# A head's attention values on TensorE: one group of eight matmuls over up to 512 queries in place of two groups, four and eight, over 256

## The reference, cut to what matters

```python
def one_block(args):                     # causal_attention, mixer B; mixer A is alike
    qb, i = args                         # 128 queries of block i
    s = jnp.einsum('bqhd,bkhd->bhqk', qb, k) * scale
    s = jnp.where((kpos[None, :] <= qpos[:, None])[None, None], s, -jnp.inf)
    pr = jax.nn.softmax(s, axis=-1)
    return jnp.einsum('bhqk,bkhd->bqhd', pr.astype(v.dtype), v)
```

## Time and profile before

| | us |
|---|---|
| median of 3 runs (1789.79 to 1790.21) | 1790.18 |
| profiled execution | 1791.9 |
| its span, first to last instruction | 1790.1 |
| PE busy in the span | 1769.0 (99%) |
| DVE busy | 1259.2 (70%) |
| ACT busy | 951.9 (53%) |
| POOL busy | 848.6 (47%) |

### The profile page before, as it was taken

How to read it: one execution, slowest core, us unless ns; L and a number is a source line. 1 busy time by engine, 2 the same in 40 slices (tenths; PEclk the granted TensorE clock), 3 DMA queues, 4 the chain that set the end, 5 groups by cost and what they waited for, 6 DMA issues and landing times.

```text
span 1790.1 us, 28924 instructions
## 1 busy us (share of the span) xinstructions
PE 1769.0 (99%) x10094; PEld 1545.7 (86%) x10094; DVE 1259.2 (70%) x2445; ACT 951.9 (53%) x1873; POOL 848.6 (47%) x458
## 2 busy tenths in 40 slices
PE   9999999999999999999999999999999999999997
PEld 9888888878879999988898888888787799999886
DVE  6279989867788888513363899897778788884133
ACT  4544877844465555422244557787444555654222
POOL 5446942354443434354434578334443434444542
PEclk9999999999999999999999999999999999999998
DMA  5332111123333333233333321111233333332431
GB/s 191 98 95 90 60 59 60 60 72 101 99 118 95 108 106 102 89 118 106 96 100 101 96 81 60 60 60 61 81 106 94 106 107 100 114 95 83 130 106 59
DMA packets 47078, 166.64 MB, mean 93 GB/s; under 512 B 5472, under 2 KB 5728, under 8 KB 46944
## 3 DMA queue, kind: packets, MB, share of 16 engines
q1 hardware_dynamic: 46080, 163.60, 29.5%
q10 hardware_dynamic: 864, 1.28, 0.2%
HBM read 162.76 MB, written 2.10 MB: 92 GB/s over the span
## 4 chain that ended last, share of the span: by engine, by line
PE 72%; issue 12%; DVE 8%; POOL 5%; ACT 2%; DMA 0%; DVEq 0%; POOLq 0%; SPq 0%; ACTq 0%
PE banks L1124 19%; PE banks L1126 18%; PE banks L1125 18%; POOL sb_wl L595 5%; PE banks L1175 3%; PE banks L1177 3%; PE banks L1176 3%; PE banks L1231 2%; PE banks L1281 2%; DVE sb_work L1613 1%; DVE sb_top L1611 1%; DVE banks L1676 1%; PE banks L1262 1%; DVE sb_pbuf L1635 1%; PE banks L1261 1%
## 5 line engine op out<-in xcount | busy, mean ns | idle before, releaser
L595 POOL TENSOR_TENSOR sb_wl<-sb_wraw,sb_wh 128x1024 fp32r<-128x1024 f32 x223 | 546.0, 2452 | 660.7 <-ACT sb_wh L723 640.9
L1124 PE MATMUL banks<-sb_xh,sb_wh 128*128 128x512 f32 (+1 forms) x1184 | 428.9, 362 | 4.0 <-POOL sb_wl L595 3.0
L1126 PE MATMUL banks<-sb_xh,sb_wl 128*128 128x512 f32 (+1 forms) x1184 | 412.0, 348 | 0.0
L1125 PE MATMUL banks<-sb_xl,sb_wh 128*128 128x512 f32 (+1 forms) x1184 | 411.5, 348 | 0.0
L723 ACT ACTIVATE sb_wh<-sb_wraw 128x1024 fp32r<-128x1024 f32 x215 | 227.2, 1058 | 298.9 <-PE banks L1126 184.5
L1124 PEld LDWEIGHTS banks<-sb_xh,sb_wh 128*128 128x128 f32 x1184 | 224.9, 190 | 30.1 <-issue 5.1
L1126 PEld LDWEIGHTS banks<-sb_xh,sb_wl 128*128 128x128 f32 x1184 | 224.4, 190 | 29.3
L1125 PEld LDWEIGHTS banks<-sb_xl,sb_wh 128*128 128x128 f32 x1184 | 225.3, 190 | 16.1
L1124 PE MATMUL banks<-sb_t_hi,sb_wh 128*128 128x256 f32 x640 | 181.2, 283 | 0.0
L1125 PE MATMUL banks<-sb_t_lo,sb_wh 128*128 128x256 f32 x640 | 181.2, 283 | 0.0
L1126 PE MATMUL banks<-sb_t_hi,sb_wl 128*128 128x256 f32 x640 | 181.2, 283 | 0.0
(11 more groups left out here) (350 smaller groups left out, 3987.0 us busy)
## 6 DMA issues: line engine op xcount, KB each, us to landing
sb_wraw<-in_weights SPq DMA_DIRECT2D x264, 512.0 KB, 3.5
sb_wraw2a<-in_weights SPq DMA_DIRECT2D x20, 512.0 KB, 3.5
sb_wraw2b<-in_weights SPq DMA_DIRECT2D x20, 512.0 KB, 4.5
sb_u<-in_x SPq DMA_DIRECT2D x8, 256.0 KB, 6.3
out<-sb_u SPq DMA_DIRECT2D x8, 256.0 KB, 2.1
sb_praw<-in_ple ACTq DMA_DIRECT2D x2, 512.0 KB, 4.3
sb_par<-in_params ACTq DMA_DIRECT2D x2, 98.5 KB, 3.1
sb_rope_tmp<-in_freq ACTq DMA_DIRECT2D x1, 24.0 KB, 4.3
```

The costliest lines, as they stand in the source:

```text
L595: nc.gpsimd.tensor_tensor(wl[:, slot(t), :], wraw[:, t % 2, :], wh[:, slot(t), :].bitcast(F32), ALU.subtract).then_inc(lo_ready, 1)
L1124: nc.tensor.matmul(out, wh_, xh_, start=start, stop=False, skip_group_check=onto)
L1125: nc.tensor.matmul(out, wh_, xl_, start=False, stop=False, skip_group_check=onto)
L1126: return nc.tensor.matmul(out, wl_, xh_, start=False, stop=stop, skip_group_check=onto)
```

## The change

A head's value work becomes one group, numbered by the head (`hd`), over all four query blocks. There is one pair of turned buffers, each of 1664 used columns, in which key block `b` holds the queries from block `b` on, next to each other: block `b` starts at column 512 x `b` and has 512 - 128 x `b` columns. So one matmul takes key block `b` with all its queries.

The group stands in slot 4 x head + 6, after the first third of the gate work and ahead of the turn of the next head's unit 0, which writes into the same buffers. ACT's copy of the group's half (step `value part`) stands where the value step was, behind the second third. The copy L781 and the low parts L1649 of a head wait until the previous head's group has been run. The copy and the addition behind the group become one each over 64 x 512 in place of two over 64 x 256. The addition's wait for `tapped` moves from head 4 to head 8.

```diff
+        head, whole = (slot - VALUE_LAG) // NT, slot >= VALUE_LAG and (slot - VALUE_LAG) % NT == NT - 1
+        if whole:
+            steps.append(("value", head))
         if TURN_LAG <= slot < UNITS + TURN_LAG:
             steps.append(("turn", slot - TURN_LAG))
         steps += [("part", p) for p in left[given + shares[0]:given + shares[0] + shares[1]]]
         if slot in PREP and PREP[slot][0] == "B":
             steps.append(("prep keys", PREP[slot]))
-        if slot >= VALUE_LAG and (slot - VALUE_LAG) % 2:
-            steps.append(("value", (slot - VALUE_LAG) // 2))
+        if whole:
+            steps.append(("value part", head))
...
-        pt_h = [sb("pt_h0", A0 + 119808, [P, 2, 256], F32R), sb("pt_h1", A0 + 99328, [P, 4, 256], F32R)]
-        pt_l = [sb("pt_l0", A0 + 121856, [P, 2, 256], F32R), idx_r[:, :, 0:256]]
-        low_part = sb("low_part", A0 + 123904, [P, 2, 256])
+        pt_h = sb("pt_h", A0 + 128000, [P, 5 * PT], F32R)
+        pt_l = sb("pt_l", A0 + 134656, [P, 5 * PT], F32R)
+        low_part = sb("low_part", A0 + 123904, [P, S])
...
+        def turned_blocks(buffer, n):
+
+            qt = n % NT
+            return buffer[:, P * qt:P * qt + PT * (qt + 1)].rearrange("p (b q) -> p b q", q=PT)[:, :, 0:P]
...
                 def turned_probabilities(n):
-                    qt, half = n % NT, n // 2 % 2
+                    qt, head = n % NT, n // NT
                     arrived("turn", n)
-                    if n >= 4:
-                        act.wait_ge(value_ready, layer * PAIRS + (n // 2 - 1))
-                    dst = pt_h[half][:, 0:qt + 1, P * (qt % 2):P * (qt % 2) + P]
+                    if head >= 1:
+                        act.wait_ge(value_ready, layer * HEADS + head)
+                    dst = turned_blocks(pt_h, n)
...
-                def value(m):
-                    hd, half = m // 2, m % 2
-                    diagonal = 2 * half + 1
-                    pe.wait_ge(prob_low, units + (2 * m + 2))
+                def value(hd):
+                    pe.wait_ge(prob_low, units + (NT * hd + NT))
...
-                    passes = [(0, pt_h), (diagonal, pt_h), (diagonal, pt_l)]
-                    passes += [(b, pt) for b in range(1, diagonal) for pt in (pt_h, pt_l)] + [(0, pt_l)]
+                    high, low = pt_h, pt_l
+                    passes = [(0, high)] + [(b, pt) for b in (3, 1, 2) for pt in (high, low)] + [(0, low)]
                     for i, (b, pt) in enumerate(passes):
-                        q0 = P if b == diagonal else 0
                         v = ukv_r[:, b, hd * P:hd * P + P] if hd < BH else idx_r[:, b, G_VA - AD:G_VA + AD]
-                        last = nc.tensor.matmul(psum[:, bank, q0:256], v, pt[half][:, b, q0:256], start=(i == 0),
-                                                stop=(i == len(passes) - 1))
+                        last = nc.tensor.matmul(psum[:, bank, P * b:S], v, pt[:, (PT + P) * b:PT * b + S],
+                                                start=(i == 0), stop=(i == len(passes) - 1))
...
                 def turned_lows(n):
-                    qt, half = n % NT, n // 2 % 2
+                    qt = n % NT
                     dve.wait_ge(turn_out, turns + (TURN_AT[("turn", n, "")] + 1))
-                    at = slice(P * (qt % 2), P * (qt % 2) + P)
+                    if n >= NT:
+                        dve.wait_ge(value_ready, layer * HEADS + n // NT)
...
-                    if slot >= NORM_LAG and (slot - NORM_LAG) % 2:
-                        combine((slot - NORM_LAG) // 2)
+                    if slot >= NORM_LAG and (slot - NORM_LAG) % NT == NT - 1:
+                        combine((slot - NORM_LAG) // NT)
```

More of the change, by code:

```diff
@@ L119 @@
 PREP |= {UNITS // 2 + 8 * p - 3: ("A", p) for p in range(AH // 2)}
-PAIRS = UNITS // 2
+HEADS = UNITS // NT
+PT = 3 * P
 Y_SPLIT = {57 + c: c for c in range(4)}
@@ L774, in turned_probabilities, with value_part @@
                 def turned_probabilities(n):
-                    qt, half = n % NT, n // 2 % 2
+                    qt, head = n % NT, n // NT
                     arrived("turn", n)
-                    if n >= 4:
-                        act.wait_ge(value_ready, layer * PAIRS + (n // 2 - 1))
-                    dst = pt_h[half][:, 0:qt + 1, P * (qt % 2):P * (qt % 2) + P]
+                    if head >= 1:
+                        act.wait_ge(value_ready, layer * HEADS + head)
+                    dst = turned_blocks(pt_h, n)
                     src = psum[:, BANK_AT[("turn", n, "")], 0:width(qt)].rearrange("p (b q) -> p b q", q=P)
                     nc.scalar.activation(dst, src, ACT.Copy).then_inc(turn_out, 1)
[L783 to L788, removed]
+                def value_part(hd):
+                    act.wait_ge(value_ready, layer * HEADS + (hd + 1))
+                    if hd >= 1:
+                        act.wait_ge(value_out, layer * HEADS + hd)
+                    own, other = (slice(0, AD), slice(AD, P))[::1 if hd % 2 == 0 else -1]
+                    nc.scalar.activation(low_part[own, :], psum[other, BANK_AT[("value", hd, "")], :],
                                          ACT.Copy).then_inc(part_out, 1)
@@ L808, in attention @@
                         exponentials(n)
-                    elif kind == "value":
+                    elif kind == "value part":
                         value_part(n)
@@ L820, in attention @@
                             act.wait_ge(turn_out, turns + (TURN_AT[("prep", ("A", 3), "")] + 1))
-                            act.wait_ge(value_out, layer * PAIRS + PAIRS // 2)
+                            act.wait_ge(value_out, layer * HEADS + BH)
                         nc.scalar.activation(yh[1][:, c], yb[:, c], ACT.Copy).then_inc(y_high, 1)
@@ L934, in _ @@
                 attention(layer, first)
-                act.wait_ge(value_out, layer * PAIRS + PAIRS)
+                act.wait_ge(value_out, layer * HEADS + HEADS)
                 for c in range(4):
@@ L1223, in bank_for @@
                         else:
-                            pe.wait_ge(value_out, layer * PAIRS + (before[1] + 1))
+                            pe.wait_ge(value_out, layer * HEADS + (before[1] + 1))
                     return BANK_AT[(kind, n, part)]
@@ L1274, in value @@
                         pe.wait_ge(va_low, layer + 1)
-                    bank = bank_for("value", m)
-                    passes = [(0, pt_h), (diagonal, pt_h), (diagonal, pt_l)]
-                    passes += [(b, pt) for b in range(1, diagonal) for pt in (pt_h, pt_l)] + [(0, pt_l)]
+                    bank = bank_for("value", hd)
+                    high, low = pt_h, pt_l
+                    passes = [(0, high)] + [(b, pt) for b in (3, 1, 2) for pt in (high, low)] + [(0, low)]
                     for i, (b, pt) in enumerate(passes):
-                        q0 = P if b == diagonal else 0
                         v = ukv_r[:, b, hd * P:hd * P + P] if hd < BH else idx_r[:, b, G_VA - AD:G_VA + AD]
-                        last = nc.tensor.matmul(psum[:, bank, q0:256], v, pt[half][:, b, q0:256], start=(i == 0),
-                                                stop=(i == len(passes) - 1))
+                        last = nc.tensor.matmul(psum[:, bank, P * b:S], v, pt[:, (PT + P) * b:PT * b + S],
+                                                start=(i == 0), stop=(i == len(passes) - 1))
                     last.then_inc(value_ready, 1)
@@ L1411, in _ @@
                         pe.wait_ge(gate_done, layer * GATES + GATES)
-                        pe.wait_ge(value_out, layer * PAIRS + PAIRS)
+                        pe.wait_ge(value_out, layer * HEADS + HEADS)
                         pe.wait_ge(yb_low, layer * 4 + 4)
@@ L1644, in turned_lows, with combine @@
                 def turned_lows(n):
-                    qt, half = n % NT, n // 2 % 2
+                    qt = n % NT
                     dve.wait_ge(turn_out, turns + (TURN_AT[("turn", n, "")] + 1))
-                    at = slice(P * (qt % 2), P * (qt % 2) + P)
+                    if n >= NT:
+                        dve.wait_ge(value_ready, layer * HEADS + n // NT)
                     src = psum[:, BANK_AT[("turn", n, "")], 0:width(qt)].rearrange("p (b q) -> p b q", q=P)
-                    v.tensor_tensor(pt_l[half][:, 0:qt + 1, at], src, pt_h[half][:, 0:qt + 1, at].bitcast(F32),
+                    v.tensor_tensor(turned_blocks(pt_l, n), src, turned_blocks(pt_h, n).bitcast(F32),
                                     ALU.subtract).then_inc(prob_low, 1)
-                def combine(m):
-                    hd, half = m // 2, m % 2
-                    dve.wait_ge(part_out, layer * PAIRS + (m + 1))
+                def combine(hd):
+                    dve.wait_ge(part_out, layer * HEADS + (hd + 1))
                     rows = slice(AD * (hd % 2), AD * (hd % 2) + AD)
-                    if hd == BH // 2 and half == 0:
+                    if hd == BH:
                         dve.wait_ge(tapped, layer * POOL_TAPS + POOL_TAPS)
```

(4 more changed lines are left out.)

## The result

The changed kernel takes 1792.79 us (median of 20 runs, 1792.16 to 1794.05) against 1790.19 us of the kernel before in the same runs: 2.6 us more, a ratio of 1.0015 with a 95% interval of 1.0009 to 1.0021. The interval leaves out 1, so the loss is real, but it lies within the forecast's bound of 0.2%, where a change counts as none. The forecast was 1790.3 us, with a range of 1785.8 to 1794.2.

What follows compares the result with a forecast made beforehand. PE's own stream was taken to bound the kernel; -3.5 us (matmuls), -3.2 (waits that go) and +6.8 (waits that come) gave +0.1, so 1790.18 becomes 1790.3 us, with an 8-in-10 range of 1785.8 to 1794.2.

Steps and rivals of the forecast that it cites:

- What bounds: Attention stage: PE's own stream sets the pace; an edit counts only by stream removed and PE waits removed or created.
- The matmuls: Value groups: eight matmuls for twelve, same columns, save 0.11 us a head, 3.5 us in all (2.9 to 4.2).
- Waits that go: Four PE waits in layer one, at heads 0 and 10 and two turns, vanish: 1.6 us, both layers 3.2 us.
- Waits that come: Before the new group PE waits for unit 3's low part, heads 0, 1, 2, 8, 10, 12: 6.8 us, both layers.
- PE's head start: PE reaches the new group 0.46 us earlier, its first group gone; ACT's and DVE's dropped work was to nearly cancel this.
- The rest: Next head's unit 0 turn, issued 0.8 us later, and other leftovers: costed at nothing.
- The sum: Whole kernel: -3.5 - 3.2 + 6.8 = +0.1 us, median 1790.18 becoming 1790.3 us.
- The gain that shows: Rival: new waits before the group hardly come, under 3.1 us in all; 1784.7 us; chance 0.22.
- The slower rival: Group late in most heads, new waits up to 7.3 us a layer, deciding from 10.3 in all; 1798.1 us; chance 0.13.

Runs made afterwards that it cites:

- the run with twelve: The changed kernel, group in its new place but cut into the twelve narrow matmuls of before: 1796.3 us, ratio to the kernel before 1.0033.
- The run with the taps moved: The changed kernel with four convolution taps moved from slots 1, 5, 9 and 13 to slots 28, 43, 58 and 62: 1789.89 us, ratio 0.9998.
- the run with shifted buffers: The changed kernel, group back behind the turn, turned buffers of odd heads starting 896 columns further on: 1786.37 us, ratio to the kernel before 0.9979.

## Why the prediction was right, point by point

The measured time lies inside the range, and the mechanism was the one forecast: less stream, old waits gone, new waits in front of the group at the places named. That it came so close was partly luck: one term was 4.0 us too small over both layers, and what went the other way left a miss of 2.5 us.

- **What bounds.** Right: every run follows PE's stream plus PE's waits, to a few tenths of a microsecond a layer.
- **The matmuls, -3.5 us.** Right, 3.5 measured by the run with twelve. By the rule of the Trainium skill that was weighed against it, TensorE: Matmul & The Clock Gate, section "Wait — 56ns, not 53.3ns?", it would be 0.3, an estimate from that page's 2.5 ns a matmul. The run decides against the rule here.
- **Waits that go, -3.2 us.** The four waits are gone from where they were, by the trace. But those in DVE's loaded stretch were in part not saved. Counted from the stage's start, PE is at head 2's group at 51.9 us (208.13 without its wait), 0.8 earlier than it was at the turn in its place (52.7), while the low part ends at 52.4 instead of 52.8: DVE has a queue of its own, and PE waits in front of the group instead, 0.69 us where I had 0 to 0.1. The run with the taps moved shows it: the wait goes when DVE's load goes.
- **Waits that come, +6.8 us.** The mechanism and the place were right, the size was not: 5.5 and 5.3 us in the two layers instead of 3.4. This is the term that was mis-sized. I held PE's head start of 0.46 us against the copy and addition that ACT and DVE lose, and let them cancel. They do so for head 8 and 10 (0.5 and 1.2 forecast, 0.61 and 1.34 measured). They don't for heads 12 and 13 (0.27 and 0 forecast, 0.65 and 0.41 measured), nor for heads 0 and 2. The run with the old groups ahead of the turn separates the place, 3.7 us, from all the rest, 2.4 more. The traces show where the rest sits: between the turn of unit 3 and the group PE takes as long in that run as in the change (2.86 us at heads 10 and 12), so PE doesn't outrun its own turn; but ACT's copy comes later behind the turn. Here are the turn and the copy at head 12, in the kernel before, the run with the old groups ahead, the change, and the run with shifted buffers:

```profile
327.06 0.60 PE L1231 MATMUL banks<-sb_ident,sb_pbuf 128*128 128x128 f32 x4
328.42 0.59 ACT L781 ACTIVATE sb_pt_h<-banks 128x512 fp32r<-128x512 f32 x1
...
328.83 0.60 PE L1236 MATMUL banks<-sb_ident,sb_pbuf 128*128 128x128 f32 x4
330.20 0.59 ACT L786 ACTIVATE sb_pt_h<-banks 128x512 fp32r<-128x512 f32 x1
...
326.70 0.60 PE L1240 MATMUL banks<-sb_ident,sb_pbuf 128*128 128x128 f32 x4
328.39 0.59 ACT L790 ACTIVATE sb_pt_h<-banks 128x512 fp32r<-128x512 f32 x1
...
324.83 0.60 PE L1242 MATMUL banks<-sb_ident,sb_pbuf 128*128 128x128 f32 x4
326.52 0.59 ACT L792 ACTIVATE sb_pt_h<-banks 128x512 fp32r<-128x512 f32 x1
```

The copy starts 1.36 and 1.37 us after the turn with the first group, 1.69 in both runs without it. ACT didn't follow the earlier PE, although its copy behind the first group was gone.

- **The rest, 0.** The later turn of unit 0 was costed at nothing. It isn't the cause at head 12: in the run with shifted buffers that turn stands ahead of the group again, and the copy is as late as in the change. At head 13 the copy starts 1.14 us after its turn in the change, 0.73 in the kernel before and 0.87 with shifted buffers; but in layer two of the change, with the same late turn, it is 0.92, so what the later turn costs there stays open. The single addition takes 0.687 us, as taken from the 64x512 row: the mean of L1665 over 32 of them, against 0.420 for each of two before. The Trainium skill, VectorE: DVE Perf Modes, section "The TRN2 errata — SBUF-src ops pay a fixed extra latency per instruction", gives (N + 151) / 0.96 ns for an fp32 addition over N columns. An estimate from it is 0.424 us for 256 columns and 0.691 for 512; this case's rows agree within 0.004.
- **The sum.** +0.1 forecast. The waits that come were 4.0 us too small over both layers, those that go 0.6 (3.8 against 3.2, by two of 0.15 us a layer that the forecast passed over) and the stream's part, by the distances of 1.39 and 1.27, 0.3; 0.6 is the open part of above: 0.1 + 4.0 - 0.6 - 0.3 - 0.6 = 2.6, as measured.
- **The rivals.** None came by its time. The gain that shows needed new waits under 3.1 us in all; there were 10.8. It came in the runs that take the waits away. The slower rival was nearer than the time says: it was to decide from 10.3 us of new waits or at ten heads, and both came, 10.8 us and ten heads a layer with idle time put down to L1656, three of them with 0.1 us or less. The time stayed within 0.2% because the other terms and the open part took 1.5 us more than the sum had for them.

## What to carry to other kernels

Before a step is moved forward in a queue whose engine never idles, list for each of its occurrences when its last input is ready and when it will be asked for; here the old trace named six heads, and a later run showed waits at just these. Work taken out ahead of the waiting step makes that engine early, and part of what it saves can come back as waiting: here the copy that it waits for came 0.3 us later behind its turn at head 12. Look at all engines of the chain for what is late: making DVE's part earlier bought nothing at head 1 and 13, where ACT's copy was late. A wait for two results can be split, the passes that need only the first going ahead: that left the group's length as it was and was worth 6.4 us.

## What the runs showed of the hardware

Two adjacent matmuls of 128 columns with weights of their own take 0.06 and 0.11 us from start to start, and the matmul behind them is 0.05 us late, whether it has 256, 384 or 512 columns. A matmul whose operand came late takes 0.10 us more to the next start (0.33 instead of 0.23 for 512 columns, 0.22 instead of 0.12 for 256), so a wait that shows as 0.5 us between starts costs 0.6. Where the bank came late it is 0.08 more (0.31 for 512 columns).
